# ScalarE takes its part of a piece at TensorE's row event instead of two events later

## The reference

```python
def _decoder_layer(x, c, k_past, v_past, q_start, params):
    mod = (jax.nn.silu(c) @ w_ada + b_ada).reshape(c.shape[0], N_MOD, D_MODEL)
    h = _rmsnorm(x, g1) * (1.0 + scale1) + shift1
    mix, k_new, v_new, gv_new = _token_mixing(h, ...)
    x = x + gate1 * mix
    h = _rmsnorm(x, g2) * (1.0 + scale2) + shift2
    x = x + gate2 * _peer_ffn(h, w_query, sub_keys, e_down, e_up)

# _token_mixing: one projection h @ w_in gives q, k, v, u, gv and two gates
    u = gelu(u); gv = _layernorm(gelu(gv), g_v, b_v)
    out_b = stick-breaking attention of q, k, v   # weights from log_sigmoid and sums over later keys
    out_a = u * (tril(w_s) @ gv + b_s)            # per chunk of 128 positions
    merged = gate_a * (out_a @ w_ba) + gate_b * (out_b @ w_bb)
    return merged @ w_out, k, v, gv

# _peer_ffn, per token and head (8 heads):
        s = einsum('nhpd,pkd->nhpk', (x @ w_query), sub_keys)   # scores of 2 x 128 keys
        top_s, top_i = top_k(s, 16)                             # of each half
        best_s, best_j = top_k(all 16 x 16 sums, 16)
        experts = 16 of 16384; gates = softmax(best_s)
        act = gelu(einsum('nd,nhkd->nhk', x, expert_down[experts]))
        out = einsum('nhk,nhkd->nd', gates * act, expert_up[experts])
```

## Time and profile before

| what | us |
|---|---|
| runs: lowest, median, highest | 2342.21, 2342.86, 2346.5 |
| the profiled execution | 2343.74 |
| its span, from the first to the last instruction | 2342.0 |
| TensorE busy (matmuls) | 1858.9 |
| VectorE busy | 1555.9 |
| GpSimd busy | 1284.8 |
| ScalarE busy | 557.2 |

### The profile page before, as it was taken

One profiled execution on the slowest core, in us unless ns is written; L12 is line 12 of the kernel. 1 busy time (PEld: TensorE's weight loads), 2 busy tenths in 40 slices (PEclk: granted clock), 3 DMA queues, 4 the chain that ended last, 5 costly groups with the idle time before them and its releaser, 6 DMA issues.

```text
span 2342.0 us, 24900 instructions
## 1 busy us (share of the span) xinstructions
PE 1858.9 (79%) x7896; PEld 1299.5 (55%) x7896; DVE 1555.9 (66%) x3451; ACT 557.2 (24%) x1184; POOL 1284.8 (55%) x1197
## 2 busy tenths in 40 slices
PE   4878889788897977979789999777665677677787
PEld 2658878667785755745667577665443222222233
DVE  1211265799878667788787565767789886776652
ACT  1041121566111221246122200110111221122121
POOL 0001044576656566667666435655566677767773
PEclk7999989889998988989987657999787899989999
DMA  8878799999999899999999798999998999999997
GB/s 290 315 278 258 268 334 354 408 357 328 382 411 412 332 402 344 412 411 351 395 410 409 288 312 299 408 394 330 388 404 324 335 386 408 391 409 408 409 409 264
DMA packets 218370, 844.78 MB, mean 361 GB/s; under 512 B 27135, under 2 KB 34615, under 8 KB 196736
## 3 DMA queue, kind: packets, MB, share of 16 engines
q0 software_dynamic: 167168, 605.66, 67.4%
q1 hardware_dynamic: 35044, 215.27, 23.9%
q10 hardware_dynamic: 16028, 22.26, 2.8%
HBM read 826.02 MB, written 16.80 MB: 360 GB/s over the span
## 4 chain that ended last, share of the span: by engine, by line
PE 39%; DMA 24%; DVE 15%; POOL 6%; issue 6%; DVEq 5%; ACT 3%; SPq 1%; ACTq 0%; POOLq 0%
PE bank L855 11%; DMA gather_ring<-in_expert_down,expert_numbers 10%; PE bank L846 9%; PE bank L1224 8%; DMA gather_ring<-in_expert_up,expert_numbers 5%; DVE expert_sums L1994 4%; DMA weight_chunks<-in_w_in 4%; DVE gather_ring L1963 4%; POOL gather_ring L811 3%; POOL gather_ring L796 2%; PE bank L1142 2%; PE bank L1139 1%; DMA v_tokens<-in_expert_up,expert_numbers 1%; DMA weight_chunks<-in_expert_down,expert_numbers 1%; DMA row_tables<-mod_prompt 1%
## 5 line engine op out<-in xcount | busy, mean ns | idle before, releaser
L796 POOL DMA_INDIRECT gather_ring<-in_expert_down,expert_numbers x510 | 588.9, 1155 | 518.3 <-DVE expert_dots L1963 259.8
L1224 PE MATMUL bank<-gather_ring,coef_diagonals 128*128 128x512 f32 x1040 | 575.6, 694 | 270.4 <-DMA gather_ring<-in_expert_up,expert_numbers 164.2
L811 POOL DMA_INDIRECT gather_ring<-in_expert_up,expert_numbers x532 | 570.4, 1072 | 312.1 <-PE bank L1224 145.3
L1963 DVE CUSTOM_DVE_ANT_0 gather_ring<-gather_ring,h_tiles 128x1024 f32<-128x1024 f32 x410 | 500.5, 1226 | 183.5 <-DMA gather_ring<-in_expert_down,expert_numbers 164.3
L1224 PEld LDWEIGHTS bank<-gather_ring,coef_diagonals 128*128 128x128 f32 x1040 | 212.0, 218 | 558.8 <-issue 418.9
L855 PE MATMUL bank<-hT,weight_chunks 128*128 128x128 f32 (+2 forms) x2304 | 401.5, 335 | 29.5 <-DMA weight_chunks<-in_w_in 21.1
L855 PEld LDWEIGHTS bank<-hT,weight_chunks 128*128 128x128 f32 x2304 | 371.7, 197 | 72.3 <-issue 36.5
L1994 DVE SCALAR_TENSOR_TENSOR expert_sums<-gather_ring,expert_coefs,expert_sums 128x1024 f32<-128x1024 f32 x269 | 345.5, 1284 | 8.6 <-issue 8.6
L846 PE MATMUL bank<-weight_chunks,hT 128*128 128x256 f32 x960 | 223.9, 393 | 25.2 <-DMA weight_chunks<-in_w_in 17.3
L846 PEld LDWEIGHTS bank<-weight_chunks,hT 128*128 128x128 f32 x960 | 188.2, 198 | 62.9 <-DMA weight_chunks<-in_w_in 20.3
L1541 ACT ACTIVATE coef_diagonals<-identity,expert_coefs 128x128 f32<-128x128 f32 x304 | 108.6, 395 | 357.6 <-DVE expert_coefs L1974 166.2
(11 more groups left out here) (268 smaller groups left out, 2154.3 us busy)
## 6 DMA issues: line engine op xcount, KB each, us to landing
weight_chunks<-in_w_in SPq DMA_DIRECT2D x84, 1024.0 KB
weight_chunks<-in_w_ada SPq DMA_DIRECT2D x24, 1024.0 KB
weight_chunks<-in_w_query SPq DMA_DIRECT2D x24, 1024.0 KB
weight_chunks<-in_w_branch_a SPq DMA_DIRECT2D x12, 1024.0 KB
weight_chunks<-in_w_branch_b SPq DMA_DIRECT2D x12, 1024.0 KB
weight_chunks<-in_w_out SPq DMA_DIRECT2D x12, 1024.0 KB
gather_ring<-in_expert_up,expert_numbers POOLq DMA_INDIRECT x532, 10.8
weight_chunks<-in_cache_k SPq DMA_DIRECT2D x16, 512.0 KB
```

The lines of the kernel that those rows point to most:

```text
L796: pool.indirect_dma_start(out=d_row(slot), out_offset=None, in_=down, in_offset=bass.IndirectOffsetOnAxis(ap=expert[:, t, h * TOPK + k:h * ...
L811: pool.indirect_dma_start(out=u_row(slot), out_offset=None, in_=up, in_offset=bass.IndirectOffsetOnAxis(ap=expert[:, t, h * TOPK + k:h * T ...
L1224: mm = nc.tensor.matmul(bank[6 + half], diag[:, n % 8, :], u_row(slot)[:, half * 512:(half + 1) * 512], start=(u == PE_TILE[t][0]), stop=( ...
L1963: nc.vector.tensor_tensor_reduce(out=row, in0=row, in1=x, scale=1.0, scalar=0.0, op0=ALU.mult, op1=ALU.add, accum_out=dots[:, m % 2, k:k + ...
```

## The change

`due_later()` adds `LATER` to the event of five kinds of pieces. The constant becomes 0, so `DUE_LATER` equals `DUE`, and ScalarE takes each piece in the event in which TensorE takes it. The other engines' programs are the same as before, word for word.

```diff
 AHEAD = 3
-LATER = 2
+LATER = 0
```

## The result

The changed kernel takes 2356.24 us (median of 7 runs, 2351.51 to 2359.05) against 2342.86 us (median of 7 runs, 2339.86 to 2354.14): ratio 1.0047, 95% interval 1.0027 to 1.0068. It is slower, by 6 to 16 us. The forecast was 2351, in a range of 2347.5 to 2356; the median lies 0.24 us beyond the end of that range and inside the outer one (2338 to 2362). The profiled execution has a span of 2356.3 us against 2342.0.

What follows compares the result with a forecast made beforehand. No engine was full: VectorE bounded 440 to 590 us, TensorE 590 to 760, plus waits between engines. Terms 9.0 - 2.9 + 5.0 - 2.9 = +8.2 us gave 2351.9, or 2351 on the runs' scale; range 2347.5 to 2356.

Steps and rivals of the forecast that it cites:

- First term: 377 to 451 us: key-score load and GELU behind one more piece make VectorE's coefficients late; +9.0 us, ends 0 and 10.6.
- the mix: At 593 us, before the merges: TensorE already waits 2.70 us for VectorE and was to wait longer.
- Second term: 864 to 876 us: a query piece comes ahead of waiting diagonals, so VectorE's combine stops waiting for TensorE; -2.9 us.
- The 8.1 us before the sum at 872 are gone: Sign of being right: TensorE's 8.12 us wait before its row sum at 871.92 us disappears.
- Third and fourth terms: Third, 1024 to 1097 us: late key-score loads, +5.0; fourth, same stretch and gv: TensorE freed of waits for ScalarE, -2.9.
- The two waits: Sample group's attention, 1024 to 1097 us: VectorE waits for late key scores twice; 3.5 and 1.5 us taken as delay.
- the 7.71 us: In gv: TensorE's wait for a ScalarE copy that stood behind new coefficients; 2.02 of it was to reach the gathers.
- GpSimd's 2.02: Soon after the gv wait: GpSimd's gather waits 2.02 us for TensorE, counted in full as gain.
- the 3.57: Sample group's attention: TensorE's 3.57 us wait for an attend piece of ScalarE behind a GELU; 0.9 counted as gain.
- Freed TensorE counts: Rival, faster: TensorE loses 19.4 us of waiting; 2323.5 if all came off the end, otherwise 2337; chance 0.16.
- No change: Rival: VectorE uses its 11.5 free us and only small terms stay; 2342.9, or 2342 on the runs' scale; chance 0.25.
- Slower still: Rival: TensorE lags VectorE in more places, most score loads come late; two more stops of 4.7 us, 2360; chance 0.16.

Runs made afterwards that it cites:

- e1: The change, with the loads of key scores for the prompt tiles' choices two events earlier in ScalarE's program; ratio 0.9996 to the kernel before.
- e2: The kernel before, no piece moved, with the loads of key scores for the prompt tiles' choices one event later; ratio 1.0067 to the kernel before.
- e3: The change, with key-score loads two events earlier and pieces due one or two events ahead of a GELU left behind it; ratio 0.9985 to the kernel before.
- e10: e9 with pieces due from event 128 on moved too, except those one or two events ahead of a GELU; ratio 0.9983 to the kernel before.
- e9: e5 with the loads of key scores two events earlier, as in e1; ratio 0.9973 to the kernel before.
- e5: The kernel before, with the change made only for pieces due from event 64 to 127; ratio 0.9983 to the kernel before.
- e6: The kernel before, with the change made only for pieces due from event 128 on; ratio 1.0024 to the kernel before.
- e7: The kernel before, no piece moved, with the loads of key scores for the prompt tiles' choices two events earlier; ratio 0.9993 to the kernel before.

## Why the prediction was right

**First term (+9.0 forecast, +10.0 measured at the merges).** Both causes stand, and the size at the merges. VectorE goes on 9.0 us after the load's issue instead of the 6.6 to 8.0 taken, so the coefficients came at 452.7 and not at 449.6 to 451.0, a lag of 12.8; by 616 us 2.8 us of that were made up. That +9.0 came so close is in part luck, since the delay was larger than priced and more of it was made up than allowed for. The GELU came at 448.4 for 448.0. The traces of e1 and e2 show that load and GELU are two causes side by side, each enough for a lag of 9 to 10 us at 616; in time e2 shows late loads to cost, and no run shows a cost of the GELU alone. The prediction treated the GELU as no later stop, which holds only while the load is late as well. The step of this term that failed is where TensorE gets the delay: not at the mix, whose wait stayed (2.60 for 2.70), but at 531 us, over ScalarE's root. The Trainium skill's page "DMA: Bandwidth & Descriptors", section "Anatomy of one DMA — SWDGE (gpsimd) path", fits 2.0 us plus the bytes over 436 GB/s to DMAs of GpSimd's path, an estimate of 2.3 us for 128 KB. The two loads measured here took 9.0 and 8.5 us from issue to VectorE's next instruction, so the fit does not carry over to them; they are ScalarE's, and no run here tests it on GpSimd's path.

**Second term (-2.9 forecast, -2.3 measured between 809 and 936 us).** The size is right, and one mechanism: the combine's wait of 2.92 us went. "The 8.1 us before the sum at 872 are gone" is wrong: 7.58 stayed, since I overlooked that the GELU of the same event stands ahead of the piece.

**Third and fourth terms (+5.0 and -2.9 forecast; +9.5 measured from 936 to 1143, -0.2 from 1143 to 1253).** The two waits came at 1052 and 1104 as priced (5.44 and 5.89 for 4.7 and 5.1). What was mis-sized is how much of them passes on: I let 5.0 of 9.8 through, on the ground that GpSimd was ahead, but the lag of the coefficients behind them grew by 3.2 and 5.1 us, 8.3 of the 11.3 waited (0.7 was made up by 1143). Another 1.9 came ahead of the first, at the coefficients of 992 us (1001 after the change), where VectorE waited 1.71 us for a GELU that I had not priced. The freed TensorE gave almost nothing: the 7.71 us and GpSimd's 2.02 behind it did go, and the waits of the kind of the 3.57 fell from 10.1 to 5.8 us in all, but the coefficients' lag fell by only 0.2. Passing on the 2.02 in full was the step that failed here; what took it up is not shown.

**The sum.** The terms measured make 10.0 - 2.3 + 9.5 - 0.2 = +17.0 us in this pair of executions, twice the +8.2 forecast; the timing says +6 to +16. From 1253 us to the end the lag falls by 2.3 more: by 6.0 up to 1475, most of it from 1324 on, where the granted clock is 0.69 for 0.66; then it grows by 3.7, which I did not trace. So the direction came from the right causes. The forecast lay low by the share of the third term that I let be swallowed (4.5 us) and by the fourth, which did not come (2.7).

**Rivals.** "Freed TensorE counts" falls by the timing, and e3 shows no gain where load and GELU are in front: 616 us is exactly where it was, and the time is within the noise. "No change" falls by the timing. "Slower still" named the right direction of the error, more delay in the late loads, but not its place: there were no further waits for key scores, the two priced ones weighed more. By the number alone the result stands between the end of the forecast (2356) and this rival (2360).

## What to carry to other kernels

In an engine's program that serves several others, an instruction is as late as the slowest engine that anything ahead of it waits for. So before work is moved forward in such a program, look for the small instructions that it passes (a load, a nonlinear function on 16 columns) and ask who waits for them: here two kinds, of 0.3 us (the loads) and 0.2 us (the GELUs), stand behind the whole delay of the first stretch, and with the loads ahead of the pieces again (e1) the kernel's loss is gone. And when a wait lands on an engine in a ring of engines that wait for each other in turn, take most of it as passed on (here 10.0 of 12.8 us and 8.3 of 11.3) unless a row shows idle time that is free to be used.

## What the runs showed that I had not expected

- Executions of one and the same program differ early: TensorE at 347 us lay 6.9 us ahead (e10) to 4.3 behind (e9) that of before, and up to there the programs of e2, e5, e6, e7, e9 and e10 are those of before. To compare two traces, count from a common row, not from the span's start.
- The load of 128 KB, issued by ScalarE, took 9.0 us (after the change) and 8.5 us (e2) from issue to use in the first stretch; the median of all these loads from issue to landing after the change is 6.6, as in the earlier trace rows.
